# Sums of squares over partitions with a constant stationary matrix, and roots and reciprocals of whole rows in PSUM, in the third block of a decoder stack

## The reference

```python
def second_block(x, ...):
    h = rmsnorm(x, norm_mix); proj = h @ w_in                 # split into all inputs of the mixers
    y_ssd = ssd_mixer(z, xbc, dt_raw, ...)                    # ends: rmsnorm(y * silu(z), norm_w), mean over 1024
    y_lru = rglru_mixer(...)
    y_ret = retention_mixer(q, k, v, ret_g)
    branch_d = einsum('bskw,kwd->bskd', [y_ssd, y_lru, y_ret], w_branch)
    merged = sum(sigmoid(gate_pre) * branch_d, over the three)
    x = x + merged @ w_o
    x = x + conv_ffn(rmsnorm(x, norm_ffn), ...)
    return rmsnorm(x, norm_final)

def retention_mixer(q, k, v, g):                              # 4 heads of value width 256
    y = retention_chunked(rotary(q), rotary(k) * d ** -0.5, v, log_gamma)
    y = y * rsqrt(mean(y * y, axis=-1) + EPS)                 # one factor for each token and head
    return y * silu(g)
```

## Time and profile before

| | us |
|---|---|
| median of 3 runs | 1416.72 (1416.09 to 1417.18) |
| profiled execution | 1418.38 |
| its span | 1416.6 |
| PE busy | 1400.9 (99%), 7808 matmul records |
| PE weight loads (PEld) busy | 1201.7 (85%) |
| DVE busy | 716.2 (51%) |
| ACT busy | 868.4 (61%) |
| POOL busy | 1185.2 (84%) |
| DMA | 256.1 MB, 181 GB/s |

### The profile page before, as it was taken

The page is one execution under the profiler, slowest core; times in us unless marked ns, Lnnn a source line. Parts: engine busy times, 40 slices in busy tenths (PEclk is TensorE's granted clock), DMA queues, the critical chain, the costliest instruction groups (busy, mean ns, idle before and its releaser), DMA issues.

```text
span 1416.6 us, 24999 instructions
## 1 busy us (share of the span) xinstructions
PE 1400.9 (99%) x7808; PEld 1201.7 (85%) x7808; DVE 716.2 (51%) x1597; ACT 868.4 (61%) x1462; POOL 1185.2 (84%) x926
## 2 busy tenths in 40 slices
PE   8999999999999999999999999999999999999998
PEld 7877778888888777788888899998899888888887
DVE  5654454655556734446555565670853612544444
ACT  6655656666675655648666676854545545755555
POOL 6877687999979777888999979899776898899895
PEclk9999999999999999999999999999999999999999
DMA  7765454666657754555666656566544565566662
GB/s 270 211 189 150 135 182 160 202 199 188 187 164 224 221 155 145 164 179 162 207 192 192 189 182 193 162 202 203 177 136 133 152 210 181 169 196 192 192 190 92
DMA packets 140336, 256.10 MB, mean 181 GB/s; under 512 B 8464, under 2 KB 99168, under 8 KB 139872
## 3 DMA queue, kind: packets, MB, share of 16 engines
q1 hardware_dynamic: 128224, 244.61, 55.8%
q10 hardware_dynamic: 12032, 10.42, 2.6%
HBM read 253.90 MB, written 1.10 MB: 180 GB/s over the span
## 4 chain that ended last, share of the span: by engine, by line
PE 92%; issue 2%; POOL 2%; DVE 2%; ACT 2%; DMA 1%; PEld 0%; ACTq 0%; POOLq 0%; PEldq 0%; DVEq 0%; SPq 0%
PE psum L1213 20%; PE psum L1214 19%; PE psum L1215 19%; PE psum L1245 17%; PE psum L1247 9%; POOL w_lo L495 1%; PE psum L1351 1%; PE psum L1332 1%; PE psum L1342 1%; PE psum L1458 1%; POOL w_lo L494 1%; DMA raw<-in_units 1%; DVE both L2077 0%; ACT w_hi L526 0%; PE psum L1779 0%
## 5 line engine op out<-in xcount | busy, mean ns | idle before, releaser
L494 POOL TENSOR_TENSOR w_lo<-raw,w_hi 128x512 fp32r<-128x512 f32 x461 | 604.2, 1311 | 215.1 <-ACT w_hi L526 205.9
L526 ACT ACTIVATE w_hi<-raw 128x1024 fp32r<-128x1024 f32 x461 | 487.0, 1058 | 299.3 <-PE psum L1215 192.7
L495 POOL TENSOR_TENSOR w_lo<-raw,w_hi 128x512 fp32r<-128x512 f32 x461 | 609.5, 1322 | 0.0
L1245 PE MATMUL psum<-both,w_hi 128*128 128x512 f32 x1040 | 259.1, 391 | 0.0
L1245 PEld LDWEIGHTS psum<-both,w_hi 128*128 128x128 f32 x1040 | 190.7, 188 | 36.7
L1213 PE MATMUL psum<-w_hi,both 128*128 128x512 f32 (+1 forms) x544 | 212.7, 391 | 2.3 <-DVE arena L2101 2.3
L1215 PE MATMUL psum<-w_lo,both 128*128 128x512 f32 (+1 forms) x544 | 206.2, 379 | 0.0
L1214 PE MATMUL psum<-w_hi,both 128*128 128x512 f32 (+1 forms) x544 | 206.2, 379 | 0.0
L1247 PEld LDWEIGHTS psum<-both,w_lo 128*128 128x128 f32 x1040 | 141.9, 190 | 10.1
L1949 DVE TENSOR_TENSOR psum<-psum,arena 128x256 f32<-128x256 f32 x136 | 58.5, 432 | 174.2 <-ACT arena L564 174.2
L1247 PE MATMUL psum<-both,w_lo 128*128 128x256 f32 x1040 | 145.0, 282 | 0.0
(11 more groups left out here) (305 smaller groups left out, 2145.2 us busy)
## 6 DMA issues: line engine op xcount, KB each, us to landing
raw<-in_units SPq DMA_DIRECT2D x453, 512.0 KB, 3.6
arena<-gate_rows ACTq DMA_DIRECT2D x8, 512.0 KB, 7.8
raw<-in_units SPq DMA_DIRECT2D x8, 384.0 KB, 3.0
arena<-in_bias ACTq DMA_DIRECT2D x2, 1024.0 KB, 5.4
arena<-acs_rows ACTq DMA_DIRECT2D x16, 128.0 KB, 4.3
arena<-in_consts ACTq DMA_DIRECT2D x1, 1296.0 KB, 5.9
raw<-in_units SPq DMA_DIRECT2D x8, 128.0 KB, 3.0
out<-arena SPq DMA_DIRECT2D x4, 256.0 KB, 2.6
```

Source lines behind the costliest of these rows:

```text
L494: pool.tensor_tensor(w_lo[s][:, 0:D // 2], raw[s][:, 0:D // 2], w_hi[s][:, 0:D // 2].bitcast(F32), ALU.subtract)
L495: pool.tensor_tensor(w_lo[s][:, D // 2:D], raw[s][:, D // 2:D], w_hi[s][:, D // 2:D].bitcast(F32), ALU.subtract)\
L526: act.activation(w_hi[s][:, :], raw[s][:, :], ACT.Copy).then_inc(hi_ready, d.inc(hi_ready))
L1245: pe.matmul(bank(4 + k), blocks_of(w_hi[s], c), both[:, 2 * c * T:2 * (c + 1) * T], start=(c == 0), stop=False, skip_group_check=True)
```

## The change

The squares become the moving operand (256 tokens wide) and a matrix of equal numbers the stationary one: `ones` (1/1024) for the SSD branch, `ones256` (1/256) for the heads. Each result is a row of 256 tokens, the same on all 128 partitions. The sums of heads 0 and 1 lie in bank 3, those of heads 2 and 3 in bank 0. ACT takes roots of whole rows in PSUM, in place: 256 columns for the SSD branch, and 512 for each pair of heads. The first pair's root moves from part 2 to part 0 of its loop, behind the last head's squares; the second pair's is in part 2. DVE takes reciprocals of whole rows in place: 256 columns for the SSD branch, where the reciprocal of two columns was, and 512 columns for each pair of heads, at the head of each call of `head_rows`, where there was one reciprocal of eight columns ahead of both. The ten spreading matmuls with their waits are gone. The diff:

```diff
--- before.py
+++ after.py
@@ -279,9 +279,9 @@
 
             return bank([0, 1, 6, 7][c % 4], c // 4 * T + lo, n)
 
-        def spread_of(col):
-
-            return rstd[:, col:col + 1].to_broadcast([P, P])
+        def head_row(h, n=1):
+
+            return bank(0 if h // 2 else 3, h % 2 * T, n * T)
 
         acs_rows = nc.dram_tensor("acs_rows", (HEADS, T), F32, kind="Internal").ap()
 
@@ -356,7 +356,7 @@
         row_ready, turn_ready, cum_ready, acs_ready = (signal(n) for n in ("row_ready", "turn_ready", "cum_ready", "acs_ready"))
         xt_ready, xdt_ready = signal("xt_ready"), signal("xdt_ready")
         acs_saved = signal("acs_saved", 16)
-        srow_ready, sbc_ready = signal("srow_ready"), signal("sbc_ready")
+        srow_ready = signal("srow_ready")
         silu_ready, cb_ready, cbm_ready = (signal(n) for n in ("silu_ready", "cb_ready", "cbm_ready"))
         seg_full = [signal(f"seg_full{b}", 16) for b in range(4)]
         seg_ready, dec_ready, m_ready, yh_ready, ys_ready = (
@@ -365,8 +365,8 @@
         act_out, prod_ready, yhi2_ready, ylo2_ready = (signal(n) for n in ("act_out", "prod_ready", "yhi2_ready", "ylo2_ready"))
         v_ready, rs_ready, rp_ready, ry_ready, ryf_ready, rsq_ready = (
             signal(n) for n in ("v_ready", "rs_ready", "rp_ready", "ry_ready", "ryf_ready", "rsq_ready"))
-        rstat_ready, rsd_ready, rrow_ready, rbc_ready, rn_ready = (
-            signal(n) for n in ("rstat_ready", "rsd_ready", "rrow_ready", "rbc_ready", "rn_ready"))
+        rstat_ready, rsd_ready, rrow_ready, rn_ready = (
+            signal(n) for n in ("rstat_ready", "rsd_ready", "rrow_ready", "rn_ready"))
         branch_out, mt_ready, mhi_ready, mlo_ready = (signal(n) for n in ("branch_out", "mt_ready", "mhi_ready", "mlo_ready"))
         merged_ready, result_dve, result_act = signal("merged_ready"), signal("result_dve"), signal("result_act")
         stored = signal("stored", 16)
@@ -1077,7 +1077,7 @@
                 gate_high(2 * h + 1)
                 if h == 0:
                     act.wait_ge(stat_ready, d.next(stat_ready))
-                    act.activation(rows[:, 0:2], bank(0, 0, 2), ACT.Sqrt, bias=small[:, 60:61])\
+                    act.activation(bank(0, 0, T), bank(0, 0, T), ACT.Sqrt, bias=small[:, 60:61])\
                         .then_inc(sd_ready, d.inc(sd_ready))
                 if h in (1, 2):
                     for q in (2 * h - 2, 2 * h - 1):
@@ -1093,10 +1093,9 @@
                 high()
                 if part == 0:
                     head_square(RET_H - 1)
-                if part == 2:
+                if part in (0, 2):
                     act.wait_ge(rstat_ready, d.next(rstat_ready))
-                    act.activation(rows[:, 0:2 * RET_H], bank(3, 0, 2 * RET_H), ACT.Sqrt, bias=small[:, 60:61])\
-                        .then_inc(rsd_ready, d.inc(rsd_ready))
+                    act.activation(head_row(part, 2), head_row(part, 2), ACT.Sqrt, bias=small[:, 60:61]).then_inc(rsd_ready, d.inc(rsd_ready))
             gate_rows()
             for y in range(4):
                 high()
@@ -1791,10 +1790,7 @@
 
             def ssd_stat(c):
                 pe.wait_ge(sq_ready, d.next(sq_ready))
-                for half in range(2):
-                    last = pe.matmul(bank(0, half, 1), a2("seg", c % 4 * T + half * P, P), ones[:, 0:1],
-                                     start=(c == 0 and half == 0), stop=(c == CH - 1 and half == 1), skip_group_check=True)
-                return last
+                return pe.matmul(bank(0, 0, T), ones, a2("seg", c % 4 * T, T), start=(c == 0), stop=(c == CH - 1))
 
             for c in range(CH):
                 if c:
@@ -1827,21 +1823,15 @@
             def ret_stat(h):
                 pe.wait_ge(rsq_ready, d.next(rsq_ready))
                 for e in range(2):
-                    for half in range(2):
-                        last = pe.matmul(bank(3, half * RET_H + h, 1), a2("seg", (h % 2 * 2 + e) * T + half * P, P), c2("hot", h * RET_H + h, 1),
-                                         start=(h == 0 and e == 0 and half == 0), stop=(h == RET_H - 1 and e == 1 and half == 1), skip_group_check=True)
-                return last
+                    last = pe.matmul(head_row(h), ones256, a2("seg", (h % 2 * 2 + e) * T, T), start=(e == 0), stop=(e == 1))
+                if h % 2:
+                    last.then_inc(rstat_ready, d.inc(rstat_ready))
 
             for h in range(RET_H):
                 linear_unit(h_hi, h_lo, free=act_free)
                 if h == 0:
                     ssd_stat(CH - 2)
                     ssd_stat(CH - 1).then_inc(stat_ready, d.inc(stat_ready))
-                if h == 1:
-                    pe.wait_ge(srow_ready, d.next(srow_ready))
-                    for half in range(2):
-                        last = pe.matmul(bank(0, half * P, P), spread_of(half), ident, start=True, stop=True)
-                    last.then_inc(sbc_ready, d.inc(sbc_ready))
                 linear_unit(h_hi, h_lo, free=act_free)
                 if h >= 2:
                     ret_stat(h - 2)
@@ -1856,16 +1846,7 @@
                     ret_stat(RET_H - 2)
                     ret_outputs(RET_H - 1)
                 if part == 2:
-                    ret_stat(RET_H - 1).then_inc(rstat_ready, d.inc(rstat_ready))
-
-            def beside_branch(part):
-                if part == 0:
-                    pe.wait_ge(rrow_ready, d.next(rrow_ready))
-                    for h in range(RET_H):
-                        for half in range(2):
-                            last = pe.matmul(bank(1 + h // 2, h % 2 * T + half * P, P), spread_of(half * RET_H + h), ident, start=True, stop=True)
-                        if h % 2:
-                            last.then_inc(rbc_ready, d.inc(rbc_ready))
+                    ret_stat(RET_H - 1)
 
             def turn_merged(first):
 
@@ -1879,7 +1860,7 @@
 
             gate_columns(act_free, beside_gates)
             pe.wait_ge(ylo2_ready, d.next(ylo2_ready, 4))
-            branch_columns(CH, act_free, beside_branch)
+            branch_columns(CH, act_free)
             gate_columns()
             branch_columns(CH)
             gate_columns()
@@ -2551,9 +2532,9 @@
                     .then_inc(rp_ready, d.inc(rp_ready))
                 if h == 0:
                     dve.wait_ge(sd_ready, d.next(sd_ready))
-                    dve.reciprocal(rstd[:, 0:2], rows[:, 0:2]).then_inc(srow_ready, d.inc(srow_ready))
+                    dve.reciprocal(bank(0, 0, T), bank(0, 0, T)).then_inc(srow_ready, d.inc(srow_ready))
                 if h == 1:
-                    dve.wait_ge(sbc_ready, d.next(sbc_ready))
+                    dve.wait_ge(srow_ready, d.made(srow_ready))
                     for c in range(CH):
                         dve.scalar_tensor_tensor(a2("xbc", c * T, T), a2("xbc", c * T, T), p2("ssd_g", c), bank(0, 0, T), ALU.mult, ALU.mult)\
                             .then_inc(hf_ready if c % 2 else vec, d.inc(hf_ready if c % 2 else vec))
@@ -2563,15 +2544,15 @@
                         dve.tensor_tensor(chunk(y_lo, CH + 2 * q, 2), a2("xbc", 2 * q * T, 2 * T), chunk(y_hi, CH + 2 * q, 2).bitcast(F32), ALU.subtract)\
                             .then_inc(ylo2_ready, d.inc(ylo2_ready))
             ret_copy(RET_H - 1)
-            dve.wait_ge(rsd_ready, d.next(rsd_ready))
-            dve.reciprocal(rstd[:, 0:2 * RET_H], rows[:, 0:2 * RET_H]).then_inc(rrow_ready, d.inc(rrow_ready))
 
             def head_rows(ys):
                 for y in ys:
                     h = y // 2
                     if y % 4 == 0:
-                        dve.wait_ge(rbc_ready, d.next(rbc_ready))
-                    dve.tensor_tensor(ar("y", y * T, T), ar("y", y * T, T), bank(1 + h // 2, h % 2 * T, T), ALU.mult)\
+                        dve.wait_ge(rsd_ready, d.next(rsd_ready))
+                        dve.reciprocal(head_row(h, 2), head_row(h, 2)).then_inc(rrow_ready, d.inc(rrow_ready))
+                        dve.wait_ge(rrow_ready, d.made(rrow_ready))
+                    dve.tensor_tensor(ar("y", y * T, T), ar("y", y * T, T), head_row(h), ALU.mult)\
                         .then_inc(rn_ready if y % 2 else vec, d.inc(rn_ready if y % 2 else vec))
                     dve.wait_ge(d.last, d.made(d.last))
                     dve.tensor_tensor(ar("y", y * T, T), ar("y", y * T, T), a2("xdt", y * T, T), ALU.mult)\
```

## The result

| | before | changed |
|---|---|---|
| median, same chip | 1416.89 us (18 runs, 1415.95 to 1418.56) | 1420.62 us (18 runs, 1419.45 to 1422.26) |
| ratio, 95% interval | | 1.0026 [1.0020, 1.0033] |
| profiled execution, its span | 1418.38, 1416.6 | 1420.81, 1419.0 |
| PE matmul records | 7808 | 7756 |

The changed kernel is 3.7 us slower: by the interval somewhat over 0.2%, small but there.

A forecast was written before the change was run, and what follows sets the result against it. PE's own stream was taken to bound the kernel; its 2.5 us saving would turn into a wait, starting unit 12 2.1 us later, plus 1.7 for the clock: 1416.7 + 3.8 = 1420.5 us, range 1417.5 to 1422.7.

The forecast's parts named there:

- PE's saving: PE, weight units counted from the gates beside the last heads: spreads gone, sums exchanged, 2.5 us ahead from unit 5.
- Roots and reciprocals: ACT roots about 0.5 us (SSD) and 0.75 (512 columns); DVE reciprocals 1.75 and 3.35 us, at 6.25 ns a column.
- The SSD reciprocal: DVE near 1065: 1.75 us, hidden in idle time with 4 us of cover.
- The first product of the second call: DVE, head rows 4 to 7: the product ACT waits for is ready 3.5 us later than before.
- PE's wait: At unit 12, PE ready at 1124.6 waits 4.6 us for POOL and starts at 1129.2, +2.1 against before.
- ACT's wait at L1090: A sign in the profile: ACT's wait for DVE's product grows from 3.9 to about 7 us.
- The clock: After PE's wait the granted clock falls to 0.50 for some three us, costing 1.7; wait and clock had chance 0.55.
- The sum: Whole kernel: 2.1 + 1.7 = +3.8 us, giving 1420.5 as median and 1422.2 profiled.
- No wait: Rival: wide reciprocal costs little more than a copy, under 1.1 us; all of -2.5 stays, 1414.2; chance 0.08.
- The clock holds: Rival: the same PE wait at unit 12 without a clock fall; +2.4 us, 1419.1; chance 0.22.
- Dearer: Rival: reciprocals a third dearer per column, or POOL and DVE slow each other longer; +2.2, 1422.6; chance 0.09.
- a rival at 0.06: Part of DVE's delay vanishes elsewhere, as in products undisturbed by POOL: 1 to 2 us less, 1417.7; chance 0.06.

The follow-up runs named there:

- e1_early: Changed kernel with both 512-column head reciprocals moved ahead of the gates, where DVE idles; 1415.44 us against 1417.20 for before, ratio 0.9983.
- e2_short: Changed kernel with 8 columns in place of 512 in both head reciprocals, same place; 1415.01 us against 1417.20 for before, ratio 0.9983.
- e9_both: e1_early with ACT's conversion of unit 12 ahead of head row 4's rounding, units 13 and 14 behind rows 4 and 5; 1415.42 us, ratio 0.9988 to before.
- e3_filler: Changed kernel with 18 unused 512-column matmuls on PE between units 11 and 12; 1419.55 us against 1417.20 for before, ratio 1.0013.
- e5_half: Changed kernel with 256 columns in place of 512 in both head reciprocals; 1418.97 us against 1416.95 for before, ratio 1.0011.
- e4_order: Changed kernel with ACT's conversions of units 12 and 13 ahead of head row 4's rounding, unit 14 behind it; 1418.24 us, ratio 1.0006 to before.
- e7_before_wide: Kernel before with an unused 512-column reciprocal at the head of each head_rows call; 1421.19 us against 1416.95 for before, ratio 1.0029.
- e8_first: Changed kernel with only the first pair's head reciprocal moved ahead of the gates; 1419.05 us against 1417.05 for before, ratio 1.0012.
- e10_second: Changed kernel with only the second pair's head reciprocal moved ahead of the gates; 1417.04 us, ratio 0.9997 to before.
- e6_ssd_only: Kernel before with the SSD branch's part of the change alone, heads as before; 1417.34 us against 1416.95 for before, ratio 1.0000.
- e11_half2: The e5_half kernel run once more for a second trace; trace +2.09 us against before.

## Why the prediction was right, step by step

- **PE's saving**, 2.5 from unit 5 on: 2.36 at the start of unit 5 and 2.48 at unit 11, and 0.76 at the start of unit 3, where 0.7 was given for its end. The chain shows the exchange as told: a sum takes 0.43 and the rotation behind it 0.43, against 0.34 and 0.54.

```profile
1036.19 0.43 PE psum L1793 x2
1036.62 0.43 PE psum L1805 x2
```

- **Roots and reciprocals.** 0.45 and 0.66 for about 0.5 and 0.75; 1.77 and 3.37 for 1.75 and 3.35. The line of 6.25 ns a column through two widths of the earlier trace rows held at a third, and PSUM made no difference. The Trainium skill, "VectorE: DVE Perf Modes", section "First, the fixed hardware budget", gives a repeat count of eight, by which I had estimated some 4.3 us; 3.37 was measured, and the measurement decides. The SSD reciprocal fits into idle time as told (3.84 us of cover, for 4).
- **The first product of the second call**, +3.5: it is ready at 1123.51, 94.18 from the mark, against 1121.43 and 91.00: +3.18. The rest is in the first call: its first gate product took 0.42 us where before shows 0.83, and so the second call begins 0.15 later, not 0.4. The same sizes then run down ACT (+3.18), POOL's start (+3.17) and its end (+3.12).
- **PE's wait**, 4.6: measured 4.29, 0.3 less as the product was. Unit 12 starts 1.81 later for 2.1.
- **ACT's wait at L1090** was put at about 7 and is 9.58. That was an error in the list of signs, without effect on the sum: the wait not only ends 3.18 later, it also begins 2.48 earlier, since ACT follows PE, and 3.92 + 3.18 + 2.48 = 9.58.
- **The clock**, 1.7: measured 1.70. At half speed that is an estimated 3.4 us at the 1.2 GHz level, for "some three". The one event that spoke for it, at 26 us, was weaker than it looked: the same wait in the same code let the clock hold in the changed kernel's own trace. The runs show the fall after 4.3, 2.3 and 2.1 us, and both outcomes at 2.9, so a chance of 0.55 against 0.22 was fair. For the changed kernel no execution of 18 reached a mean clock of 1.000. Before did in 43 of 81, the kernels in whose traces PE doesn't wait for POOL (e1_early, e2_short, e9_both) in 10 of 32, and the filled wait of e3_filler in 2 of 10.
- **The sum**, +3.8: +3.55 in the trace, +3.73 in the medians. The predicted 1420.5 met 1420.62 with errors of -0.3 us in the wait and nothing larger, so it isn't right by two faults that cancel. The profiled time was put at 1422.2 and was 1420.81. There the start point was off: the changed trace reaches its mark 1.10 us earlier than the trace of before, which alone of the two lost some 1.7 us to the clock at 26 us. 3.55 - 1.10 is the 2.4 us by which the spans differ.
- **The rivals.** "No wait" would have needed a reciprocal under 1.1 us; e2_short, at 0.22 us, shows that it then goes that way (-2.12, for the -2.5 less units 12 to 14). "The clock holds" is e3_filler's trace, +2.24 for +2.4. "Dearer" adds up to 1422.7 rather than 1422.6, without effect. What I hadn't seen is the coupling in the first call: I counted the product undisturbed by POOL for the second call only and left more of that to a rival at 0.06. The expectation that built on a shorter first reciprocal missed by that (e5_half), and that of e4_order by the same coupling in the second call, which made unit 15 late.

What stays open: how much of the time the clock falls after 1.3 to 3 us of wait. Mean clocks of 1.000 were had by 1 of 6 executions of e7_before_wide, 1 of 10 of e5_half, 2 of 10 of e8_first, 3 of 10 of e4_order, 4 of 10 of e10_second; but e1_early, without any such wait, had 2 of 11: a fall at 14 or 26 us lowers the mean as well, and these counts are too few to draw a curve.

## What to carry to other kernels

An edit that takes work from the bounding engine and lays wider work on another is worth what the next hand-over allows: follow the new work along the in-order queues until it reaches the bounding engine again, and price the wait from the moment at which that engine, now earlier, is ready. Then look for a stretch in which the other engine idles and its inputs are already there: the same 6.7 us of reciprocals cost 5.7 us in one place (3.55 + 2.13) and nothing in the idle stretch ahead of it. Behind a new wait add a second term for the clock, and give it a chance, not a certainty.

## What the hardware showed beyond the expectation

- **DVE and POOL hinder each other, depending on operands.** A product of two SBUF operands on DVE, 256 columns, takes 0.42 to 0.43 us with POOL idle and 1.07 to 1.25 with POOL at work (L2558 and L2560 above); the product beside it that has one operand in PSUM takes 0.41 to 0.42 either way. POOL's halves go from 1.30 to 1.48. The Trainium skill, "SBUF — State Buffer", section "Who interferes with whom", says that a DVE instruction with two SBUF inputs contends with a GpSimd instruction that reads SBUF, and that with at most one SBUF input, outside the 2-port modes, it doesn't; both rows agree. So a step that makes DVE earlier can make it slower: half of a reciprocal (1.6 us) taken from the first call gained nothing.
- **The same wait left the clock alone in one execution and halved it in the next**: 2.87 us and 2.82 for the unit behind it, 2.86 us and 4.29. A wait of 1.31 us left it alone in its trace. At 26 us, where the code is the same in all kernels, PE idles 1.35 or 1.36 us in ten of the thirteen traces: the clock fell behind it in six (before, e1_early, e6_ssd_only, e7_before_wide, e10_second, e11_half2) and held in four (changed, e4_order, e5_half, e8_first). In the other three it had fallen at 14 us, behind a wait of 0.80, and the later wait is 0.93 or 0.94. The length of the wait alone doesn't decide it.
- **A slow unit hides what comes behind it.** With the clock held (e3_filler), units 12 to 14 each lose 0.1 us to POOL's longer halves; with the clock fallen in unit 12 POOL gets ahead, and in the changed kernel units 13 and 14 lose 0.04 in all. So the fall costs 1.3 us by both pairs of traces (3.55 - 2.24, 2.09 - 0.77), where its own unit shows 1.5 to 1.7.
